# Neighbourhood attention of a fused two-block kernel: the position bias moves from a matmul on TensorE to an addition in PSUM on VectorE

## The reference

```
col_start = jnp.clip(cols - NA_WIN_COLS // 2, 0, GRID_W - NA_WIN_COLS)
col_in = (cols[None, :] >= col_start[:, None]) & (cols[None, :] < col_start[:, None] + NA_WIN_COLS)
...
bias = rpb[:, dr_idx[None, :, None], dc_idx[:, None, :]]
s_lat = jnp.einsum('bhqd,bhrkd->bhqrk', q_r, k_s, preferred_element_type=jnp.float32) * scale + bias.astype(jnp.float32)
s_lat = jnp.where(col_in[:, None, :], s_lat, -jnp.inf).reshape(B, H, GRID_W, wr * GRID_W)
s_ctx = jnp.einsum('bhqd,bhcd->bhqc', q_r, k_ctx, preferred_element_type=jnp.float32) * scale
p = jax.nn.softmax(jnp.concatenate([s_lat, s_ctx], axis=-1), axis=-1).astype(v.dtype)
```

## Time and profile before

| | |
|---|---|
| runs of the kernel before | 2199.41, 2203.15, 2206.08 us |
| span of the profiled execution | 2203.0 us |
| its own time beside the span | not given apart from the runs above |
| mean granted TensorE clock | 0.964 of full speed |
| TensorE matmul busy | 1987.3 us, 14122 records |
| VectorE busy | 588.5 us, 1120 records |
| ScalarE busy | 423.4 us, 778 records |
| GpSimd busy | 206.2 us, 183 records |
| from HBM | 661.08 MB, 301 GB/s over the span |

### The profile page before, as it was taken

One profiled execution on the slowest core, in us unless ns is written; L12 is line 12 of the kernel. 1 busy time (PEld: TensorE's weight loads), 2 busy tenths in 40 slices (PEclk: granted clock), 3 DMA queues, 4 the chain that ended last, 5 costly groups with the idle time before them and its releaser, 6 DMA issues.

```text
span 2203.0 us, 32618 instructions
## 1 busy us (share of the span) xinstructions
PE 1987.3 (90%) x14122; PEld 1389.8 (63%) x14122; DVE 588.5 (27%) x1120; ACT 423.4 (19%) x778; POOL 206.2 (9%) x183
## 2 busy tenths in 40 slices
PE   8999899887888888887898887999999999999997
PEld 3857575643455556653565543756888876588886
DVE  6766310124212000000002103353432044640001
ACT  2222221222202000000001212444200032630001
POOL 0730000020000000000000000334000002700000
PEclk9999999999999999999999998999999999999999
DMA  9958899999999999999999998531686743044450
GB/s 365 372 199 343 339 420 424 417 427 426 421 426 427 423 418 426 420 425 426 421 425 426 416 423 343 140 116 39 222 294 199 180 144 116 1 153 153 129 158 20
DMA packets 181383, 664.24 MB, mean 302 GB/s; under 512 B 17432, under 2 KB 121401, under 8 KB 142649
## 3 DMA queue, kind: packets, MB, share of 16 engines
q1 hardware_dynamic: 181240, 662.16, 76.7%
HBM read 661.08 MB, written 1.05 MB: 301 GB/s over the span
## 4 chain that ended last, share of the span: by engine, by line
PE 58%; DMA 30%; DVE 5%; ACT 4%; issue 1%; POOL 1%; SPq 1%; ACTq 0%; DVEq 0%; POOLq 0%
PE ps L1213 19%; PE ps L692 11%; DMA ring<-in_w_up 8%; DMA ring<-in_w_gate 7%; DMA ring<-in_w_down_slots 7%; DMA ring<-in_context_weights 6%; PE ps L1663 5%; PE ps L1689 2%; PE ps L1048 2%; PE ps L1012 2%; PE ps L1323 2%; DMA arena<-in_w_ada 2%; PE ps L1222 2%; PE ps L1568 1%; ACT arena L2605 1%
## 5 line engine op out<-in xcount | busy, mean ns | idle before, releaser
L1213 PE MATMUL ps<-arena,ring 128*128 128x256 f32 x1984 | 429.9, 379 | 1.0 <-DVEq L392 0.9
L1213 PEld LDWEIGHTS ps<-arena,ring 128*128 128x128 f32 x1984 | 376.5, 190 | 54.2 <-issue 1.7
L1663 PE MATMUL ps<-ring,arena 128*32 128x256 f32 x4000 | 260.5, 407 | 76.2 <-DMA ring<-in_w_up 43.4
L692 PE MATMUL ps<-arena,ring 128*128 128x256 f32 (+1 forms) x1392 | 319.2, 390 | 6.5 <-DMA ring<-in_context_weights 6.5
L692 PEld LDWEIGHTS ps<-arena,ring 128*128 128x128 f32 (+1 forms) x1392 | 256.0, 190 | 76.3 <-DMA ring<-in_context_weights 23.4
L1663 PEld LDWEIGHTS ps<-ring,arena 128*32 128x32 f32 x4000 | 125.4, 115 | 194.9 <-DMA ring<-in_w_up 59.4
L2311 ACT ACTIVATE arena<-ps 128x512 f32<-128x512 f32 (+4 forms) x147 | 78.2, 532 | 739.7 <-PE ps L692 326.8
L1689 PE MATMUL ps<-ring,arena 128*32 128x512 f32 x1024 | 136.9, 660 | 54.4 <-DMA ring<-in_w_down_slots 50.6
L1689 PEld LDWEIGHTS ps<-ring,arena 128*32 128x32 f32 x1024 | 29.0, 114 | 141.1 <-DMA ring<-in_w_down_slots 87.0
L3116 POOL TENSOR_TENSOR XC<-XC,arena 128x256 f32<-128x256 f32 x32 | 23.4, 730 | 986.0 <-ACT XC L2406 965.7
L692 PE MATMUL ps<-ring,arena 128*128 128x256 f32 (+3 forms) x320 | 87.6, 425 | 0.0
(11 more groups left out here) (387 smaller groups left out, 1982.6 us busy)
## 6 DMA issues: line engine op xcount, KB each, us to landing
ring<-in_w_down_slots SPq DMA_DIRECT2D x64, 2048.0 KB, 14.5
ring<-in_w_up SPq DMA_DIRECT2D x63, 2048.0 KB, 13.6
ring<-in_w_gate SPq DMA_DIRECT2D x62, 2048.0 KB, 14.1
ring<-in_w_ada SPq DMA_DIRECT2D x27, 2048.0 KB, 9.6
ring<-in_w_ffn_in SPq DMA_DIRECT2D x44, 1024.0 KB, 7.7
ring<-in_context_weights SPq DMA_DIRECT2D x35, 1024.0 KB, 14.7
ring<-in_w_ffn_out SPq DMA_DIRECT2D x16, 1408.0 KB, 7.4
ring<-in_w_in SPq DMA_DIRECT2D x9, 2048.0 KB, 11.6
```

Of the source, the lines that this page charges most:

```text
L692: m = mm(o, a, x, start=(k == 0 and r == 0), stop=(k == kt - 1 and last))
L1213: m = mm(b, w[:, k, c:c + P], src[:, k, :], start=(k == 0), stop=(k == kt - 1))
L1663: m = mm(b[u][32 * c:32 * c + 32, T * x:T * x + T], xs[:, 2 * h + k, CAP * e:CAP * e + CAP], w[:, k, at_:at_ + T], start=(h == 0 and k == ...
```

## The change

The bias is brought in unreversed: the host now stores it once for each of the 64 grid columns, so that each partition reads one run of 64 x 42 floats, and `flip64` is gone from the tables. The queries are negated as they are written (by -0.125), so the scores come out of TensorE with the opposite sign; GpSimd makes mask minus bias (`outside` is +1e30 outside the window). The matmul L1149 is gone. VectorE takes the minimum over the context half of a unit's columns, and then one instruction adds mask minus bias to the latent half in PSUM and takes the minimum of that and of the first one; exp has the scale -1. The wait for `ww_ready` moves from TensorE to VectorE, ahead of the first `largest`. The grouped-query units are as before.

```diff
@@ TensorE
-                pe.wait_ge(ww_ready, l + 1)
...
-                            m = mm(b[:], q[:, P * qt:P * qt + P], k[:, keys], start=True, stop=(kind == "ga"))
...
-                        if kind == "na":
-                            for name, b, e in both:
-                                at_ = 7 * (2 * hp + e) + 3 - 2 * qt
-                                close_bank(mm(b[:, xo:xo + T], tb2("flip64"), WW[:, at_:at_ + 4, :], start=False, stop=True), name)
+                            close_bank(mm(b[:], q[:, P * qt:P * qt + P], k[:, keys], start=True, stop=True), name)
@@ ScalarE
-                    step(a(Pr[n % 8], b[:], ACT.Exp, scale=1.0,
+                    step(a(Pr[n % 8], b[:], ACT.Exp, scale=-1.0 if UNITS2[n][0] == "na" else 1.0,
@@ VectorE
-                    step(ts(naq[:, i, :], t, b[:, T + 1:T + 2], 0.125, ALU.add, ALU.mult), frees=f"rq{i}x{l}")
+                    step(ts(naq[:, i, :], t, b[:, T + 1:T + 2], -0.125, ALU.add, ALU.mult), frees=f"rq{i}x{l}")
...
+                dve.wait_ge(ww_ready, l + 1)
+
                 def largest(n):
-                    b = read_bank(dve, f"sc{n}{N}")
-                    step(v.tensor_reduce(nm[:, n % 8:n % 8 + 1], b[:], AX.X, ALU.max, negate=True), nm_ready[X])
+                    kind, hp, qt, e = UNITS2[n]
+                    b, least = read_bank(dve, f"sc{n}{N}"), nm[:, n % 8:n % 8 + 1]
+                    if kind == "ga":
+                        step(v.tensor_reduce(least, b[:], AX.X, ALU.max, negate=True), nm_ready[X])
+                        return
+                    own, of_ctx = b[:, T * (1 - l):T * (2 - l)], ctx_least[:, n % 8:n % 8 + 1]
+                    step(v.tensor_reduce(of_ctx, b[:, T * l:T * l + T], AX.X, ALU.min))
+                    bias = at(24064 + 64 * (7 * (2 * hp + e) + 3 - 2 * qt), T)
+                    step(v.tensor_tensor_reduce(out=own, in0=own, in1=bias, scale=1.0, scalar=of_ctx, op0=ALU.add, op1=ALU.min, accum_out=least), nm_ready[X])
@@ GpSimd
-                step(nc.gpsimd.tensor_tensor(WW[:, 1:42, :], WW[:, 1:42, :], bc(tb2("neg_col"), 1, 41, 64), ALU.add), ww_ready)
+                step(nc.gpsimd.tensor_tensor(WW[:, 1:42, :], bc(tb2("outside"), 1, 41, 64), WW[:, 1:42, :], ALU.subtract), ww_ready)
@@ SP
-                        src_ = bass.AP(I["rpb"].tensor, (l * 42) * P, [[1, 64], [P, 42 - half], [1, 64]])
-                        sp.dma_start(WW[64 * half:64 * half + 64, half:42, :], src_).then_inc(s_ww, 16)
+                        sp.dma_start(WW[64 * half:64 * half + 64, half:42, :], I["rpb"][l, :, 0:42 - half, :]).then_inc(s_ww, 16)
@@ host
-    a["rpb"] = np.ascontiguousarray(np.pad(rpb, ((0, 0), (0, 0), (48, P - 79))))
+    rpb = np.pad(rpb, ((0, 0), (0, 0), (48, P - 79)))
+    a["rpb"] = np.stack([rpb[:, :, 63 - q:P - 1 - q] for q in range(64)], 1)
```

More of the change, by code:

```diff
@@ L69 @@
            ("eps", 1), ("ln_eps", 1), ("pick", 8), ("token", 2), ("fold", 16), ("eps64", 1)]
-TABLES2 = [("half64", 128), ("flip64", 128), ("neg_col", 64), ("rope_c", 256), ("rope_s", 256),
+TABLES2 = [("half64", 128), ("outside", 64), ("rope_c", 256), ("rope_s", 256),
            ("rope_r", 128), ("gla_lv", 160), ("diag32", 32), ("gla_bd", 256)]
@@ L110, in tables @@
     t["half64"] = (i[:, None] // 64 == i[None, :] // 64)
-    t["flip64"] = (i[:, None] // 64 == i[None, :] // 64) & (i[:, None] % 64 + i[None, :] % 64 == 63)
     c = np.arange(64)
     c0 = np.clip(c - 8, 0, 48)
-    t["neg_col"] = np.tile(np.where((c[None] >= c0[:, None]) & (c[None] < c0[:, None] + 16), 0, NEG)[::-1], (2, 1))
+    t["outside"] = np.tile(np.where((c[None] >= c0[:, None]) & (c[None] < c0[:, None] + 16), 0, -NEG), (2, 1))
     inv = 10000.0 ** (-np.arange(16, dtype=np.float32) / 16)
@@ L294, in build @@
         rawt = at(7152, 4, T)
-        GA, cc = at(2000, 8), at(2008, 4)
+        GA, cc, ctx_least = at(2000, 8), at(2008, 4), at(2016, 8)
         ctx_x = [XC[:, :, 0:T], XC[:, :, T:2 * T]]
@@ L1127, in latent @@
                 keys = slice(T * l, T * l + 2 * T)
-                xo = T * (1 - l)
                 def scores(j):
@@ L1134, in scores @@
                     for qt in range(2):
-                        both = []
                         for e in range(2):
@@ L1141, in scores @@
                             q, k = (naq[r, hp], nak[r, hp]) if kind == "na" else (gaq[r, hp], gak[r, int((2 * hp + e) // 3 != e)])
-                            m = mm(b[:], q[:, P * qt:P * qt + P], k[:, keys], start=True, stop=(kind == "ga"))
-                            both.append((name, b, e))
-                            if kind == "ga":
-                                close_bank(m, name)
-                        if kind == "na":
-                            for name, b, e in both:
-                                at_ = 7 * (2 * hp + e) + 3 - 2 * qt
-                                close_bank(mm(b[:, xo:xo + T], tb2("flip64"), WW[:, at_:at_ + 4, :], start=False, stop=True), name)
+                            close_bank(mm(b[:], q[:, P * qt:P * qt + P], k[:, keys], start=True, stop=True), name)
                 def turn(n):
```

## The result

The changed kernel takes 2207.81 us (median of 13 runs, 2204.86 to 2214.01) against 2201.77 for the kernel before on the same chip (13 runs, 2195.15 to 2206.08): ratio 1.0031, 95% interval 1.0021 to 1.0041, so 4.6 to 9.0 us slower. The forecast was 2203.7 in a range of 2196 to 2209.5, most likely within 0.3% of the kernel before. The time lies in the range, on its slow side; the loss of 0.31% lies just past the 0.3%, which its interval includes. That it lies in the range is partly luck: the kernel before took 2201.77 here and not the 2203.15 from which the forecast started, and 1.0031 times that would be 2210.0, just outside. The sum had a loss of 0.55 us and left out most of what was measured.

What follows compares the result with a forecast made beforehand. No single engine bounds it: four engines pass each 128-query unit round a ring, read by its chain of waits. Layer 0 gains 0.56 us, layer 1 loses 1.11; 2203.15 + 0.55 gives about 2203.7, range 2196 to 2209.5.

Steps and rivals of the forecast that it cites:

- The sum: Both attention stages together: 0.56 us gained in layer 0 and 1.11 lost in layer 1, so 0.55 us lost.
- my replay: Old unit times of both attention stages shifted: 0.56 us gained in layer 0, 1.1 lost in layer 1.
- The unit's duration: VectorE's two instructions per neighbourhood unit, with gaps: 1.09 us where it was 0.72.
- Layer 1: Second attention stage, where VectorE was already late: exp 4 late by 0.47 us, 1.1 us lost in all.
- From unit 12 on nothing changes: Later units of each attention stage are the other attention, unchanged, paced by VectorE and ScalarE.
- exp 4 0.7 gained: Layer 0's stage: unit 4's maximum ends at 1470.7, so its exp starts then instead of at 1471.39.
- Rival 3: TensorE's clock halves after idling before layer 0's second scores: exp 4 1 to 2 us later, about 2205.5; within the forecast's 0.74.
- The slope of 16: Some eight places per layer where the new instruction's length counts in full: 16 us per us of T.
- T: Length of VectorE's new add-and-minimum instruction: taken as 0.60 us, between 0.425 and 0.88.
- Rival 1: All removed work on the chain in both attention stages comes back, 6.6 us: 2196.6, or 2190.4 at most; chance 0.13.
- Rival 4: The stall at 1429.4, before everything changed, may go or come elsewhere: 4.1 us either way; within the forecast's 0.74.
- Edits at nothing: GpSimd's masking, the moved wait, the bias DMA, negated queries and exp's scale: no cost, done well before the scores.

Runs made afterwards that it cites:

- e3: Kernel before with 12 small products (48 TensorE instructions) ahead of layer 0's run of 32x32 products; its ratio puts it at 2198.3 us.
- e2: Kernel after with 12 small products (48 TensorE instructions) ahead of layer 0's run of 32x32 products; 2196.3 us, ratio 0.9986 to the kernel before.
- e6: e2 with the gated layer's squares product repeated, 6 more times in layer 0 and 3 in layer 1, filling TensorE's idle gaps; ratio 0.9988.
- e7: e2 without the position bias: VectorE takes one minimum over 512 elements per neighbourhood piece instead of two instructions; ratio 0.9980.
- e1: Kernel after with a small 32-column product ahead of each of layer 0's 12 neighbourhood score pieces, restoring 48 TensorE instructions; ratio 1.0061.
- e5: e2 with a product of the removed one's size ahead of each neighbourhood score, overwritten by the scores; no total time given.

## Why the prediction held, and where its sum did not

The ledger is the start of each exp, counted from the start of its stage, which repeats within 0.03 us between the kernels as they were and those with 48 ahead (us, e3 to e2; then my replay):

```
             layer 0: e3     e2     change   replay    layer 1: e3     e2     change   replay
exp 0            3.77   3.54   -0.23                       3.78   3.54   -0.24
exp 4           12.68  12.76   +0.08    -0.70             11.62  11.92   +0.30    +0.47
exp 8           20.92  21.41   +0.49    -0.70             19.62  20.61   +0.99    +0.97
exp 12          28.86  29.43   +0.57    -0.56             27.56  28.64   +1.08    +1.11
exp 20          44.71  45.29   +0.58                      43.41  44.49   +1.08
```

- **The unit's duration**: 1.05 for 1.09. Right.
- **Layer 1**: +1.04 for +1.11, and right at exp 8 and exp 12; exp 4 was 0.17 better than replayed.
- **From unit 12 on nothing changes**: right in both layers (0.57 at exp 12, 0.58 at exp 20).
- **Layer 0, the step that failed**: "exp 4 0.7 gained" came out at 0.08 lost. The timeline of the kernel after shows both halves:

```profile
1466.61 3.78 PE L1138 MATMUL ps<-arena 64*128 64x512 f32 x8 [4.18 <-ACT arena L2300]
...
1468.76 1.28 ACT L2594 ACT_TABLE_LOAD   x1 [2.21 <-PE ps L1138]
1470.06 0.69 ACT L2594 ACTIVATE arena<-ps,arena 128x512 f32<-128x512 f32 x1
...
1478.71 0.69 ACT L2594 ACTIVATE arena<-ps,arena 128x512 f32<-128x512 f32 x1 [1.85 <-DVE arena L3014]
```

  The scores of unit 4 ran at half clock, and the table load waited for them. Rival 3 stood ready for this with 1 to 2 us, and a clock under 1.00 between 1465 and 1480 was on my list of signs of being wrong. TensorE was to be idle for 3.8 us there; the row has 4.18. e6's rows put the price at 0.96. I gave it no share in the central sum. The rest, 0.4 us, came at exp 8: I had it hold its gain, but ScalarE waits 1.85 us there for VectorE, which had its rotation's last part and a longer unit in hand. That TensorE's wait before exp 8 would go and be put down to VectorE instead was right.
- **The slope of 16** was mis-sized: 8 by e7 against e2. At exp 4 of layer 1 the longer unit costs 0.86, not the five times 0.33 that I counted; between the first maxima VectorE waits for exps, and part of the extra time falls into these waits. (At T = 0.425 this slope gives a gain of 2.3 us, not the 3 that the prediction names; its 1.4 didn't rest on that.)
- **Rival 1, that the 6.6 us on the chain come back**: the 6.6 us were real rows, worth 1.04 us when taken out alone (e7 against e3). What stands on a chain is what was waited for, not what the next one in line would let you gain.
- **Rival 4, the stall**: its mechanism is what moved the total most. I priced it at 4.1 us "either way" (3.82 came) and gave it nothing in the sum, as if its place could not be known. It can: with a block of 256 instructions and the count of removed ones, it can be computed. A removed product counts two instructions, with its weight load, on each of its two passes: 12 products of layer 0 are 48.
- **Edits at nothing**: the mask, its wait and the bias DMA cost nothing that shows; packets under 512 bytes fell from 17,432 to 6,807 and nothing on the chain can be put down to that.

Of the 4.0 us between the two spans the stall is 3.8 and attention 1.6, less the 1.4 by which the first stage happened to begin earlier. The medians differ by 6.0 us; 5.4 of these are accounted for by the stages, and the rest is inside the interval.

## What to carry to other kernels

A piece on the chain of waits is worth only the distance to the next late engine: replay the ring of engines unit by unit, as in layer 1, before you price it. When an edit adds or removes instructions ahead of a fast burst on the same engine, count them against the size of a packet of the instruction stream, and judge the edit on kernels where the stall is out of the way. Look where an engine waits for another right before work that nobody needs yet: swapping these two gave 8.8 us, five times the 1.7 that the change costs.

## What the hardware showed that I had not expected

- TensorE's own program stalls it: 1.68 to 3.60 us at the same place modulo 256 instructions, in runs of 192 small products. Of the three places two were moved by 48 or 208 instructions; the first, in all 14 kernels, was left as it is.
- Less work lowers the clock: without the product TensorE is idle for 4.18 us in layer 0 (timeline of the kernel after) and the granted clock falls to 0.50, where it never fell with the product and 2.3 us of idleness. In layer 1 of e2 it falls at 1879.2 with no idle stretch over 1.74 us in the 16 us of the stage before. Part of the TensorE time that the edit frees (12.7 us of records, 5.0 us on the page) is used up by slower products: the 48 score records of layer 0 are busy for 18.3 us where it was 15.2.
- Two 64-row scores side by side take 1.06 us together, and 1.05 each with another product between them, be it of 32 columns (e1) or of 256 (e5).
